# A hybrid decoder step on one core: HGRN outer products by groups of 32 partitions, modulation tiles and sample read-outs in another order, decayed states on ScalarE

## The reference, cut to what matters

```python
def step(S, inp):
    qc, kc, vc, lf = inp
    G = jnp.cumsum(lf, axis=2)
    Gl = G[:, :, -1]
    o_inter = jnp.einsum('bhik,bhkv->bhiv', qc * jnp.exp(G), S)
    diff = G[:, :, :, None, :] - G[:, :, None, :, :]
    decay = jnp.exp(jnp.where(mask, diff, -jnp.inf))
    A = jnp.einsum('bhik,bhjk,bhijk->bhij', qc, kc, decay)
    o = o_inter + jnp.einsum('bhij,bhjv->bhiv', A, vc)
    S = S * jnp.exp(Gl)[..., None] + jnp.einsum('bhjk,bhjv->bhkv', kc * jnp.exp(Gl[:, :, None, :] - G), vc)
    return S, o
```

## Time and profile before

| | |
|---|---|
| three runs, median (lowest to highest) | 2317.75 us (2316.18 to 2320.46) |
| profiled execution, its own time | 2314.56 us |
| its span | 2309.3 us |
| TensorE busy over the span | 2239.2 us (97%) |
| VectorE, ScalarE, GpSimd busy | 1498.0 (65%), 1268.5 (55%), 1091.6 us (47%) |
| HGRN block, layer 0 (first instruction to the next block's first) | 151.48 to 194.65: 43.17 us |
| HGRN block, layer 1 | 1288.61 to 1331.43: 42.82 us |

### The profile page before, as it was taken

One profiled execution on the slowest core, in us unless ns is written; L12 is line 12 of the kernel. 1 busy time (PEld: TensorE's weight loads), 2 busy tenths in 40 slices (PEclk: granted clock), 3 DMA queues, 4 the chain that ended last, 5 costly groups with the idle time before them and its releaser, 6 DMA issues. The chain is left out here.

```text
span 2309.3 us, 57987 instructions
## 1 busy us (share of the span) xinstructions
PE 2239.2 (97%) x20556; PEld 2070.7 (90%) x20556; DVE 1498.0 (65%) x3064; ACT 1268.5 (55%) x2439; POOL 1091.6 (47%) x990
## 2 busy tenths in 40 slices
PE   7999999999999999999999999999999999999998
PEld 4967779999998899999989586899999988999997
DVE  3876339943226878888668663599322297887885
ACT  3652225576557855555556422455765596555554
POOL 0231018864446656566304110498444474665661
PEclk8999999999999999999999999999999999999999
DMA  7472135555554289899544802455555634998993
GB/s 291 156 251 98 58 137 182 175 200 184 186 190 147 96 266 308 276 309 312 196 169 153 297 5 103 148 184 181 198 188 185 196 108 134 315 311 274 311 306 129
DMA packets 124246, 457.09 MB, mean 198 GB/s; under 512 B 13792, under 2 KB 14304, under 8 KB 122976
## 3 DMA queue, kind: packets, MB, share of 16 engines
q1 hardware_dynamic: 105696, 388.37, 48.0%
q0 software_dynamic: 18432, 67.12, 10.5%
HBM read 450.94 MB, written 4.49 MB: 197 GB/s over the span
## 5 line engine op out<-in xcount | busy, mean ns | idle before, releaser
L462 POOL TENSOR_TENSOR parts<-ring,parts 128x512 fp32r<-128x512 f32 x358 | 464.1, 1299 | 470.1 <-ACT parts L455 455.3
L455 ACT ACTIVATE parts<-ring 128x512 fp32r<-128x512 f32 x616 | 387.5, 633 | 349.9 <-PE ps_u L509 281.3
L505 PE MATMUL ps_u<-h_parts,parts 128*128 128x256 f32 x4096 | 563.8, 280 | 1.1 <-ACT parts L455 0.6
L2766 PE MATMUL ps_y<-act_parts,parts 128*128 128x256 f32 x4096 | 562.5, 279 | 0.0
L505 PEld LDWEIGHTS ps_u<-h_parts,parts 128*128 128x128 f32 x4096 | 514.7, 188 | 3.8 <-ACT parts L455 2.3
L2766 PEld LDWEIGHTS ps_y<-act_parts,parts 128*128 128x128 f32 x4096 | 514.8, 188 | 0.8 <-ACT parts L2696 0.7
L462 DVE TENSOR_TENSOR parts<-ring,parts 128x512 fp32r<-128x512 f32 x258 | 185.3, 724 | 359.9 <-ACT parts L455 337.6
L2817 POOL TENSOR_TENSOR act_parts<-big,act_parts 128x256 fp32r<-128x256 f32 x256 | 246.3, 962 | 303.0 <-ACT act_parts L2795 303.0
L509 PE MATMUL ps_u<-h_parts,parts 128*128 128x256 f32 x2048 | 323.0, 279 | 1.0 <-DVE parts L462 0.7
L2770 PE MATMUL ps_y<-act_parts,parts 128*128 128x256 f32 x2048 | 322.6, 279 | 0.0
L509 PEld LDWEIGHTS ps_u<-h_parts,parts 128*128 128x128 f32 x2048 | 275.3, 188 | 2.0 <-DVE parts L462 1.1
(11 more groups left out here) (412 smaller groups left out, 2818.5 us busy)
## 6 DMA issues: line engine op xcount, KB each, us to landing
ring<-in_stream SPq DMA_DIRECT2D x503, 512.0 KB, 4.2
more_ring<-in_stream SPq DMA_DIRECT2D x126, 512.0 KB
extra_ring<-in_stream SPq DMA_DIRECT2D x32, 512.0 KB, 6.5
mod_ring<-in_stream SPq DMA_DIRECT2D x32, 512.0 KB, 3.3
big<-in_stream SPq DMA_DIRECT2D x16, 512.0 KB, 11.6
ring<-in_lead SPq DMA_DIRECT2D x6, 512.0 KB, 3.4
out_state_out<-big SPq DMA_DIRECT2D x2, 1440.0 KB, 6.9
big<-in_state SPq DMA_DIRECT2D x2, 1280.0 KB, 8.1
```

Source lines behind the costliest of these rows:

```text
L455: eng.activation(m.parts[:, q % PARTS, 0, :], half_tile(m, t, half), ACT.Copy).then_inc(s["hi_ready"], 1)
L462: eng.tensor_tensor(m.parts[:, q % PARTS, 1, :], half_tile(m, t, half), m.parts[:, q % PARTS, 0, :].bitcast(F32), ALU.subtract).then_inc(m ...
L505: pe.matmul(out, hi[:, k, :], hr[:, side, kk, 0:tokens], start=(kk + side == 0), stop=False)
L2766: pe.matmul(ps[:, half * KD // 2 + k, :], hi[:, k, :], act_parts[:, j % AHEAD, side, :], start=False, stop=False)
```

## The change

Five things are changed, all in `hgrn_block`.

1. Outer products by groups. GROUP is 32 // C = 4 blocks. `mask_v(tt)` makes only 4 copies for 128 tokens, with a mask in which block j of every 32 partitions is kept. A matmul then takes 32 partitions of keys as weights (32x64) and 256 columns of values: 4 groups, 2 pairs and 2 halves, 16 matmuls for 128 tokens. Each group writes to a PSUM bank of its own. The calls are `products(0, 0, 4)`, `products(1, 0, 2)` and `products(1, 2, 4)`.
2. The sample read-outs stand in two halves behind distances 2 and 3; `read_states` works in 8 calls of 4 blocks.
3. The modulation tiles stand in runs of one to four in other places; the turns of their rows, too; `turn(3)` stands behind the last read-out, and 4 matmuls of `keep_busy` behind that.
4. The masked values of the samples have a buffer of their own, and no mask waits for TensorE any more.
5. The decayed sample states are made by ScalarE, 16 instructions of 128x64, and not by GpSimd.

```diff
+    GROUP = 32 // C
...
-            def mask_v(turn):
...
-                for b in range(TB // 2):
-                    i = act.activation(vm[0:n, turn % 2, :, b, :], values, ACT.Copy, scale=mask[0:n, first + b:first + b + 1])
+            def mask_v(tt):
...
+                for j in range(GROUP):
+                    i = act.activation(vm[:, tt, :, j, :], values, ACT.Copy, scale=m.mix("block_rows")[:, j:j + 1])
...
             act.wait_ge(s["kt_out"], 3)
             mask_v(0)
+            mask_v(1)
             copy_rows(act, m, s, ada_rows, ps_mod, 1)
             copy_columns(act, m, s, ps_mod, 1, 1)
-            mask_v(1)
-            mask_v(2)
-            mask_v(3)
+            mask_samples()
+            for pair in range(A_PAIRS):
+                for b in range(NB):
+                    t = NP + NS * b + NS - 1
+                    i = act.activation(m.states[:, pair, 1 + b, :], m.state0[:, pair, b, :], ACT.Copy,
+                                       scale=since[:, pair, t:t + 1])
+                i.then_inc(s[f"kept{pair}"], 1)
             copy_rows(act, m, s, ada_rows, ps_mod, 2)
             copy_columns(act, m, s, ps_mod, 2, 2)
-            mask_v(4)
...
-                pool.tensor_tensor(m.states[:, pair, 1:, :], m.state0[:, pair, :, :], last, ALU.mult).then_inc(
-                    s[f"kept{pair}"], 1)
...
-            def products(step):
-                pe.wait_ge(s["vm_ready"], step + 1)
+            def products(tt, first, end):
+
+                pe.wait_ge(s["vm_ready"], tt + 1)
                 for pair in range(A_PAIRS):
-                    if step >= 2:
-                        pe.wait_ge(s[f"after{pair}"], HALF * (step - 1))
...
+                    if tt:
+                        pe.wait_ge(s[f"after{pair}"], GROUP * end)
+                for pair in range(A_PAIRS):
+                    for group in range(first, end):
+                        tokens = slice(32 * group, 32 * group + 32)
+                        for r in range(2):
+                            rows = slice(r * HD, (r + 1) * HD)
+                            mm = pe.matmul(ps_outer[rows, group, pair * GROUP * HD:(pair + 1) * GROUP * HD],
+                                           ktt[tokens, tt, pair, rows], vm[tokens, tt, 2 * pair + r, :, :], start=True, stop=True)
+                mm.then_inc(s["u_ready"], 1)
...
-            read_samples()
-            ada(16, 20)
...
             turn(2)
...
-            read_states(0)
-            ada(24, 27)
...
+            ada(24, 26)
+            read_states(1, 1)
...
+            read_states(3, 0)
+            read_states(3, 1).then_inc(s["inter_ready"], 1)
             turn(3)
-            mm = read_states(3)
-            mm.then_inc(s["inter_ready"], 1)
+            keep_busy(pe, m, ps_outer[:, 3, :], 4)
...
-    const("block_rows", j // 8 == np.arange(P // 8)[None, :])
+    const("block_rows", j // 8 % 4 == np.arange(P // 8)[None, :] % 4)
```

More of the change, by code:

```diff
@@ L1216, in _ @@
             act.activation(m.states[:, 0:A_PAIRS, 0, :], after[:, :, BLOCKS - 1, :], ACT.Copy)
-        @block.gpsimd
-        def _(pool):
-            for pair in range(A_PAIRS):
-                last = blocks(since, True, NS - 1, NS)[:, pair, :, :].broadcast_to([P, NB, HD])
-                pool.tensor_tensor(m.states[:, pair, 1:, :], m.state0[:, pair, :, :], last, ALU.mult).then_inc(
-                    s[f"kept{pair}"], 1)
+            copy_rows(act, m, s, ada_rows, ps_mod, 3)
+            copy_columns(act, m, s, ps_mod, 3, 3)
         @block.tensor
@@ L1249, in inter, with read_samples @@
                 return pe.matmul(out[rows], state[rows], qt[rows, pair, t:t + n], start=True, stop=True)
-            def read_samples():
-                pe.wait_ge(s["sample_free"], 1)
-                for b in range(NB):
+            def read_samples(first, end):
+                for b in range(first, end):
                     for pair in range(A_PAIRS):
@@ L1258, in read_samples, with read_states @@
                                        m.state0[:, pair, b, :])
-                mm.then_inc(s["sample_read"], 1)
-            def read_states(turn):
+                return mm
+            def read_states(turn, half):
+                first = turn * HALF + half * GROUP + 1
                 for pair in range(A_PAIRS):
-                    pe.wait_ge(s[f"after{pair}"], HALF * (turn + 1))
-                for b in range(turn * HALF + 1, min((turn + 1) * HALF + 1, BLOCKS)):
+                    pe.wait_ge(s[f"after{pair}"], first + GROUP - 1)
+                for b in range(first, min(first + GROUP, BLOCKS)):
                     for pair in range(A_PAIRS):
@@ new lines, in products, with sample_products @@
+                mm.then_inc(s["u_ready"], 1)
+            def sample_products(pair):
+                pe.wait_ge(s["vm_ready"], 3)
+                for other in range(A_PAIRS):
+                    pe.wait_ge(s[f"after{other}"], TB + GROUP * (pair + 1))
+                for r in range(2):
+                    rows = slice(r * HD, (r + 1) * HD)
+                    mm = pe.matmul(ps_outer[rows, pair, :], ktt[0:NB * NS, 2, pair, rows],
+                                   vms[0:NB * NS, 2 * pair + r, :, :], start=True, stop=True)
+                mm.then_inc(s["samples_u"], 1)
@@ L1372, in _ @@
             ve.sem_inc(s["values_done"], 1)
-            for turn in range(4):
-                ve.wait_ge(s["u_ready"], 2 * turn + 2)
-                for b in range(turn * HALF, (turn + 1) * HALF):
+            for first, ready in ((0, 1), (TB, 2), (TB + HALF, 3)):
+                ve.wait_ge(s["u_ready"], ready)
+                for b in range(first, TB if ready == 1 else first + HALF):
                     for pair in range(A_PAIRS):
-                        new, j = after[:, pair, b, :], b % HALF
-                        add = ps_outer[:, (2 * turn + pair) % 4, j * HD:(j + 1) * HD]
+                        new = after[:, pair, b, :]
+                        add = ps_outer[:, b // GROUP % 4, (pair * GROUP + b % GROUP) * HD:(pair * GROUP + b % GROUP + 1) * HD]
                         if b == 0:
```

74 lines of the change are left out of this document (35 added, 39 removed).

## The result

The changed kernel takes 2332.4 us (median of 10 runs, 2325.52 to 2336.77); the kernel before took 2317.74 beside it (10 runs, 2315.86 to 2322.45). The ratio is 1.0056, with an interval of 1.0045 to 1.0066: 14.7 us slower, where 11 us faster was forecast. The profiled execution took 2333.28 us with a span of 2331.2; its TensorE is busier in sum than before, for a kernel that gives it less to do.

What follows compares the result with a forecast made beforehand. TensorE's own program was taken to set the length of both HGRN blocks. Terms of -4.0 us a layer (-8.0) and -3.0 for the clock behind them sum to -11.0, taking 2317.75 to 2306.7 us, range 2300 to 2315.

Steps and rivals of the forecast that it cites:

- Distance 0: Block start: without GpSimd beside VectorE, distance 0 starts at about 152.95 and not 154.11, -1.15 us a layer.
- Row groups: Outer products: tiles of 32 rows run side by side, 3.0 us instead of 7.48, -4.45 us a layer.
- rivals 1 and 2: Outer products: row groups don't run side by side, 7.5 us (0.13), or wait for each other, 10 us (0.08).
- the slower one: Outer products: row groups wait for each other to the last column, 10 us a layer, 2323.8 us; chance 0.08.
- The turn: Turn 1, now right behind its tile, waits for ScalarE's copy: +0.5 us a layer.
- the tile behind it: The next tile behind turn 1, tile 16, waits for ScalarE's columns: +0.43 us.
- the ScalarE states: Decayed sample states on ScalarE: 16 instructions of 0.26 us, 4.2 us, costing nothing if early enough.
- TensorE's end: Block end: TensorE ends about 1.5 us after the last read-out, later than VectorE; sum +0.1 us a layer.
- rival 4: Block as forecast, clock behind it kept in neither layer, 2309.7, or both, 2303.7 us; chance inside the forecast's 0.70.
- the block's terms: Inside the HGRN block: outer products, start, turns, changes of shape and end, -4.0 us a layer, -8.0 for two.
- The clock behind the block: Delta block's opening: full clock kept is worth 3.1 us a layer, even chance each, one counted, -3.0 us.

Runs made afterwards that it cites:

- e1_pads: The changed kernel with four bf16 matmuls of 256 columns, results unread, behind seven of the eight groups of read-outs: 2314.77 us, ratio 0.9992.
- e14: The changed kernel with four bf16 matmuls of 256 columns behind the first three read-outs alone: 2315.15 us, ratio 0.9994.
- e13: The changed kernel with eight fp32 matmuls of 64x64 on 8 columns, alternating upper and lower rows, behind seven read-outs: 2345.98 us, ratio 1.011.
- e8: The changed kernel with two bf16 matmuls of 256 columns behind each of seven read-outs: 2327.99 us, ratio 1.005.
- e5: The changed kernel with 28 bf16 matmuls of 256 columns all behind the first of the read-outs: 2319.7 us, ratio 1.0007.
- e12: The changed kernel with six bf16 matmuls of 256 columns behind each of seven read-outs: 2317.26 us, ratio 0.9989.
- e3: The kernel before with outer products by groups of 32 partitions alone, with the masked copies they need: 2324.68 us, ratio 1.0029.
- e2: The changed kernel with outer products again by matmuls of 128 partitions and 512 columns (wrong sums): 2327.37 us, ratio 1.0037.
- e7: The changed kernel with four bf16 filler matmuls behind all read-outs, sample halves included, and eight 512-column matmuls at the end: 2316.51 us, ratio 0.9992.
- e11: The kernel before with ScalarE states, last turn and four matmuls after the last read-out, four filler matmuls behind its first three read-outs: 2314.56 us, ratio 0.9972.
- e4: The kernel before with the decayed sample states on ScalarE alone: 2317.59 us, ratio 0.9993.
- e9: The changed kernel with 16 fp32 matmuls of 64x64 on 8 columns, on one array quarter, behind seven read-outs: 2382.28 us, ratio 1.0273.
- e6: The kernel before with only the last turn moved behind the last read-out and four 512-column matmuls behind it: 2314.47 us, ratio 0.9985.

## Why the prediction was wrong

**What held.** Distance 0 started 1.34 us behind the block's start instead of 2.63 (forecast: 1.15 less). Row groups ran side by side: 1.05 us for the first call (forecast 1.0), and 1.02 to 1.03 for half as many (at full clock in e1_pads, 173.83 to 174.85), where I had 1.0. So rivals 1 and 2, both on the row groups, were wrong, the slower one too: it had the right sign by a mechanism that isn't there. The turn waited 0.50 us, the tile behind it 0.32, the ScalarE states took 3.92 us (forecast 4.2). TensorE's end was as drawn. One tile waited 0.41 us.

**The sum of these can be checked.** In e14 layer 0 the block is 43.41 us long. Its filler takes 1.5 us (0.54, 0.54 and 0.44); 3.4 us of it at the start are at half clock and cost 1.7 too much, the last 2.5 us about 1.0 (not all of it is TensorE's work). That leaves 39.2 us, worked out, and the forecast had 39.2. The block at full clock is what I said it would be; that it agrees to a tenth is luck.

**The step that failed** is the one under the clock: every term inside the block was taken at 2.4 GHz, because the earlier trace rows had 1.00 and 0.99 there, and the clock was weighed only for the stretch behind it. What the runs showed in its place: inside the block the clock was a margin, and the change spent it. What had kept it isn't shown piece by piece; the old outer products (7.5 us of 512-column matmuls on the whole depth of the array) and long runs of the same kind are what the change took away. 31.4 us of layer 0's block went at 1.2 GHz; the block of 39.2 became 53.3. Half of the 31.4 would be 15.7, and 14.1 were lost: 0.85 us of the stretch are holes, and small matmuls take less than double at the low clock (16 read-outs 1.81 us from start to start, against 1.03).

The forecast with the clock kept inside the block and never behind it was 2309.7 us (rival 4). Against that, with the price of the filler by its rows for both layers, the rest is what the clock takes or gives:

| kernel | filler, us | 2309.7 + filler | measured | rest |
|---|---|---|---|---|
| changed kernel | 0 | 2309.7 | 2332.4 | +22.7 |
| e13, thin, seven places | 7.4 | 2317.1 | 2346.0 | +28.9 |
| e8, two each, seven places | 4.3 | 2314.0 | 2328.0 | +14.0 |
| e5, 28 in one place | 6.3 | 2316.0 | 2319.7 | +3.7 |
| e14, four each, first three | 3.0 | 2312.7 | 2315.2 | +2.5 |
| e1, four each, seven places | 7.4 | 2317.1 | 2314.8 | -2.3 |
| e12, six each, seven places | 10.4 | 2320.1 | 2317.3 | -2.8 |

(The kernel before took 2317.7 to 2320.5 on these chips, so a rest of 3 us is no finding.) The base 2309.7 has the time outside the span of the kernel before; all seven kernels take some 3.2 us less there, a term that the forecast put at nothing. With it each rest is 3.2 larger: +25.9 for the changed kernel, +5.7 for e14, +0.9 for e1, +0.4 for e12. So the 14.7 us are the clock's 25.9, less the 8.0 that the block's terms gained and less these 3.2, a gain that I hadn't forecast. The cost goes to nothing once the filler is dense and stands at all seven places, and most of it is gone with the first three. Which part of the change let the clock fall isn't shown. Row groups alone take 2324.7 us against the 2309 that their term gives, but with a hole of over 2 us ahead of the first fall in both layers (e3); the new order with dense products takes 2327.4, and falls in mid-block in one layer of its profile (e2).

**The clock behind the block.** I gave an even chance a layer and 3.1 us. The size held: 6.75 us of opening become 3.80 and 3.81 where the clock is kept (e7, e11), 2.9 less. The chance was too high for this kernel: kept in neither layer of the changed kernel, of e1 or of e14, and its term, -3.0, was 0. The Trainium skill (TensorE: Matmul & The Clock Gate, HAM oscillation — how this bites in real kernels) ties the fall to gaps in TensorE's work. The changed kernel's trace disagrees: from the block's start to the fall at 172.97 no gap is over 0.50 us, e1_pads holds the clock over the two holes of turn 1, and e4's falls with no hole over 0.2; only e3's falls behind 2.18 and 2.54 us fit it. By that rule I could have cleared the inside of the block; by the runs, only a look at what the matmuls are made of could have warned me.

**Where I could have seen it.** The earlier trace rows show the clock falling at about 194.2, behind read-outs, a turn and 1 us of the block's last hole. I wrote that row down as a thin stretch with a hole behind it, and then made a thin stretch at 169 to 182 without asking the same question there. A rival "the clock falls inside the block", from half of the 30 us behind the first read-outs, was there to be priced: +15 us a layer.

**What stays open:** how dense is dense enough (number type, rows and columns of the filler were not separated), which part of the change is to blame, whether e3's late tile or its thin work let the clock fall, what shortens the time outside the span by some 3 us, and why in the changed kernel's profile the clock doesn't come back before 210.5, where e1_pads's first fall is over after 3 to 3.5 us.

## What to carry to other kernels

Where the granted clock is 1.00 all through a busy stretch, it is a condition of the forecast and not a constant: before counting matmuls taken off TensorE as time gained, ask what will be left between them, and price the case that the clock falls there, at half of the rest of the stretch. A kernel with small tiles and few columns may owe its clock to the dense work that one is about to shrink; a few full-array matmuls in the thin part (here four at each of three places, 0.54 us a place) are a cheap test of it and can be the cure. A control by filler has to be measured for its own length first, as e9 shows. And where times differ by a few us, compare the spans too: 3.1 of e6's 3.5 us lie outside them.

## What the runs showed of the hardware

- Filler of equal length, 0.54 us at seven places a layer: 128x128 tiles with 256 bf16 columns held the clock at 1.00 (2314.8 us), 64x64 tiles with 8 fp32 columns did not (2346.0 us).
- The clock stayed at 1.2 GHz for the last 31 us of the block with TensorE at work for 97% of them, and came back in the next block at 210.5.
- It fell at 191.5 in e4 with no hole over 0.2 us since the block's start, and held over one of 1.13 us in the kernel before.
- 16 matmuls of 64x64 on 8 fp32 columns took 1.9 us on one quarter of the array; 16 that take turns between quarters took 1.03.
- Row groups of 32 with 64 columns run side by side in fp32: the sums of 16 blocks in 1.05 us, against twice 1.87 by 512-column matmuls of the full depth.
- Two layers of one execution, with the same program, fall at different places (e14: 40.9 us into the block, and 37.5), and the executions of some kernels lie further apart than those of others: 21.3 us in e8, 5.2 in e12.
- The time outside the span is 4.9 to 5.6 us for the kernel before and e4, and 1.8 to 3.3 for all others here.
